# Scan mixer of a two-model stack: where its last tables and the first gated-layer weights are kept, vector additions placed between scan steps, and another tile order in the gated layer

## The reference, cut to what matters

```python
def s5_mixer(h, ...):
    u = h.reshape(b, s, 64, 16)                      # 64 groups of 16 channels
    y = y_fwd(u) + y_bwd(u) + d_skip * h             # two linear recurrences, 64 complex states per group
    g = gelu(y)
    val, gate = split(g @ w_glu, 2)                  # w_glu: 1024 x 2048
    return val * sigmoid(gate)
```

## Time and profile before

| | |
|---|---|
| time, median of 3 | 3243.75 us (3242.51 to 3245.97) |
| the profiled execution | 3244.16 us, of it the span 3242.4 us |
| PE busy | 2956.9 us (91%) |
| DVE, ACT, POOL busy | 1552.6, 1088.2, 233.1 us |
| mean granted PE clock | 0.939 of full speed |

### The profile page before, as it was taken

How to read it: one execution, slowest core, us unless ns; L and a number is a source line. 1 busy time by engine, 2 the same in 40 slices (tenths; PEclk the granted TensorE clock), 3 DMA queues, 4 the chain that set the end, 5 groups by cost and what they waited for, 6 DMA issues and landing times.

```text
span 3242.4 us, 39114 instructions
## 1 busy us (share of the span) xinstructions
PE 2956.9 (91%) x15982; PEld 2386.7 (74%) x15982; DVE 1552.6 (48%) x2302; ACT 1088.2 (34%) x1665; POOL 233.1 (7%) x216
## 2 busy tenths in 40 slices
PE   6999997479999989989999799998999998898977
PEld 5787887467888777787787478887788886665745
DVE  5776664734434334534434554344543344534444
ACT  4332333333222225525435232222332223422233
POOL 2333220100000000000000300000100000100000
PEclk9999998789999989989999799999999999987868
DMA  3244547343443221122221322222122222111000
GB/s 111 88 143 159 165 133 238 124 139 106 136 117 117 78 92 58 53 87 74 82 82 69 130 91 91 102 94 78 66 91 102 93 92 86 53 40 40 15 26 27
DMA packets 109956, 305.40 MB, mean 94 GB/s; under 512 B 27488, under 2 KB 67872, under 8 KB 80464
## 3 DMA queue, kind: packets, MB, share of 16 engines
q1 hardware_dynamic: 104656, 281.40, 26.4%
q10 hardware_dynamic: 5120, 21.50, 1.7%
HBM read 265.20 MB, written 41.85 MB: 95 GB/s over the span
## 4 chain that ended last, share of the span: by engine, by line
PE 80%; DVE 8%; ACT 3%; issue 2%; POOL 1%; DMA 1%; SPq 0%; DVEq 0%; ACTq 0%; POOLq 0%
PE ps L94 79%; DVE s_ L121 2%; PE ps L99 2%; DVE H_ L121 1%; DVE htf_ L135 1%; ACT htf_ L117 0%; ACT wh_ L117 0%; ACT hh_ L117 0%; DVE ol_ L121 0%; DVE Pm_ L121 0%; DVE nmx_ L143 0%; SPq L158 0%; ACT R_ L117 0%; DVE R_ L121 0%; DVE R_ L135 0%
## 5 line engine op out<-in xcount | busy, mean ns | idle before, releaser
L94 PE MATMUL ps<-hh_,wh_ 128*128 128x512 f32 x2184 | 870.2, 398 | 31.3 <-DVE wl_ L121 14.1
L94 PE MATMUL ps<-hl_,wh_ 128*128 128x512 f32 x2184 | 856.0, 392 | 0.0
L94 PE MATMUL ps<-hh_,wl_ 128*128 128x512 f32 x2184 | 855.1, 392 | 0.0
L121 DVE TENSOR_TENSOR wl_<-raw_,wh_ 128x2048 fp32r<-128x2048 f32 x209 | 480.3, 2298 | 558.2 <-ACT wh_ L117 558.1
L117 ACT ACTIVATE wh_<-raw_ 128x2048 fp32r<-128x2048 f32 x209 | 398.9, 1909 | 367.7 <-PE ps L94 339.7
L94 PEld LDWEIGHTS ps<-hh_,wh_ 128*128 128x128 f32 x2184 | 413.3, 189 | 131.3 <-DVE wl_ L121 14.2
L94 PEld LDWEIGHTS ps<-hh_,wl_ 128*128 128x128 f32 x2184 | 413.2, 189 | 88.1
L94 PEld LDWEIGHTS ps<-hl_,wh_ 128*128 128x128 f32 x2184 | 413.7, 189 | 87.4 <-issue 3.7
L94 PE MATMUL ps<-ah_,wl_ 128*128 128x512 f32 x704 | 279.5, 397 | 0.0
L94 PE MATMUL ps<-ah_,wh_ 128*128 128x512 f32 x704 | 278.3, 395 | 0.0
L94 PE MATMUL ps<-al_,wh_ 128*128 128x512 f32 x704 | 277.7, 395 | 0.0
(11 more groups left out here) (320 smaller groups left out, 3702.4 us busy)
## 6 DMA issues: line engine op xcount, KB each, us to landing
raw_<-in_w SPq DMA_DIRECT2D x209, 1024.0 KB, 4.9
sO<-s5ce_ SPq DMA_DIRECT2D x32, 256.0 KB, 4.0
sW<-s5wt_ SPq DMA_DIRECT2D x16, 512.0 KB, 3.7
sA<-os_ SPq DMA_DIRECT2D x24, 256.0 KB, 2.1
ol_<-sA SPq DMA_DIRECT2D x24, 256.0 KB, 3.7
sT<-sK SPq DMA_DIRECT2D x32, 128.0 KB, 3.5
sB<-mk_ SPq DMA_DIRECT2D x8, 510.0 KB, 7.6
wh_<-sW ACTq DMA_DIRECT2D x3, 1024.0 KB, 6.6
```

Source lines behind the costliest of these rows:

```text
L94: return self.e.matmul(out, lhsT, rhs, start=start, stop=stop, skip_group_check=True)
L121: return Nothing() if self.e is None else self.e.tensor_tensor(out, a, b, op)
```

## The change

It has four parts.

1. Tables 16 to 19 lie in slots 2 and 0 (`place_of`), where the lag tables 10, 11 and the tables 12, 13 were. Tables 18 and 19 are so loaded only after outputs(0) and outputs(1), by two transfers that ACT issues between its state copies. Each unit of the gated layer goes one slot further (first unit: slot 1).
2. SP loads the first two weight units into `raw0` and `raw1` as soon as same(0) and same(1) have read them, ahead of all `yx` and `yb` transfers.
3. DVE runs the first four `U` additions between the single steps of half 1: after 8, 5, 5 and 5 steps. ACT runs Gelu 0 and 1 ahead of the state copies of un = 4; Gelu 2 and 3 come behind the copies of un = 6 and 7; the two weight splits move too.
4. In the gated layer each output tile m takes value tiles k = 0..6, gate tiles k = 0..6, value tile 7, gate tile 7; the host lays the weights out in that order. Before it was value 0..7, gate 0..7. Both banks are waited for at the start of m.

```diff
+def place_of(i):
+    return i % 8 if i < 16 else i - 14
 def table_load(K, ac, i, *free):
-        ac.wait_ge(*K.at("s.used", i - 8))
+        ac.wait_ge(*K.at("s.used", i - 8 if i < 16 else i - 6))
...
 def s5_tensor(K, pe):
+        parts = [(n, b, k) for ks in (range(7), (7,)) for n, b in (("gv", bv), ("gt", bg)) for k in ks]
+        for (u, j), (name, b, k) in zip(pe.tiles(16), parts):
...
+            pe.wait_ge(*K.at("s.gl", k))
...
 def s5_scalar(K, ac, g, nxt):
-        table_load(K, ac, 16 + un)
+        if un > 1:
+            table_load(K, ac, 14 + un)
...
+        if un in (2, 3):
+            table_load(K, ac, 16 + un)
+        for n in {3: (0, 1), 6: (2,), 7: (3,)}.get(un, ()):
+            s5_gelu(K, ac, n)
+        if un == 5:
             ac.upto = len(K.units) - 1
-            ac.wait_ge(*K.at("s.used", 13))
+            ac.wait_ge(*K.at("s.used", 15))
             high(K, ac, ac.unit)
...
-    ac.wait_ge(*K.at("s.used", 15))
+    ac.wait_ge(*K.at("s.used", 17))
     high(K, ac, ac.unit + 1)
...
 def s5_vector(K, dv, g, nxt):
-    while at[1] < 64:
-        step(1)
-    bias_vector(K, dv)
     for un in range(8):
+        if un < 4:
+            for _ in range(8 if un == 0 else 5):
+                if at[1] < 64:
+                    step(1)
+        if un == 4:
+            while at[1] < 64:
+                step(1)
+            bias_vector(K, dv)
+            s5_gelu_low(K, dv, 0)
+            s5_gelu_low(K, dv, 1)
...
 def s5_sync(K, sp):
+    sp.upto = len(K.units) - 1
+    for n in range(2):
+        sp.wait_ge(*K.at("s.used", 8 + n))
+        load(K, sp, sp.unit + n)
...
-        if un in (5, 6):
-            sp.upto = len(K.units) - 1
-            sp.wait_ge(*K.at("s.used", 11 + un))
-            load(K, sp, sp.unit + un - 5)
...
-        K.slot[u] = (u - (K.first_glu if u >= K.first_glu else 0)) % SLOTS
+        K.slot[u] = (u - (K.first_glu - 1 if u >= K.first_glu else 0)) % SLOTS
```

More of the change, by code:

```diff
@@ L1087 @@
 NT = 20
+def place_of(i):
+    return i % 8 if i < 16 else i - 14
 def table(K, i):
     w = [t[:, :].bitcast(F32) for n in (2, 0, 1) for t in (K.wh[n], K.wl[n])]
-    return ([K.raw[0][:, :], K.raw[1][:, :]] + w)[i % 8]
+    return ([K.raw[0][:, :], K.raw[1][:, :]] + w)[place_of(i)]
 def table_load(K, ac, i, *free):
@@ L1105, in table_load @@
         ac.wait_ge(*K.at("p.sW", 2 * n + 1))
-    ac.dma(table(K, i), K.d[name][n]).then_inc(*K.lane(f"table{i % 8}").up("s.raw", i))
+    ac.dma(table(K, i), K.d[name][n]).then_inc(*K.lane(f"table{place_of(i)}").up("s.raw", i))
 def tables_early(K, ac, m):
@@ L1196, in s5_tensor @@
         outputs(un)
-    rhs = lambda k: (K.hh[:, k, :], K.hl[:, k, :], ("s.gl", k))
     for m in range(8):
@@ L1201, in s5_tensor @@
         pe.wait_ge(*K.after(pe, K.gb, "gv", m))
-        gemm(K, pe, bv, rhs, 8)
-        pe.mark("gv", m)
         pe.wait_ge(*K.after(pe, K.gb, "gt", m))
-        gemm(K, pe, bg, rhs, 8)
-        pe.mark("gt", m)
+        parts = [(n, b, k) for ks in (range(7), (7,)) for n, b in (("gv", bv), ("gt", bg)) for k in ks]
+        for (u, j), (name, b, k) in zip(pe.tiles(16), parts):
+            h, l = K.w(u, j)
+            if j == 0:
+                pe.wait_ge(*K.at("lo", u))
+            pe.wait_ge(*K.at("s.gl", k))
+            pe.mm(b, h, K.hh[:, k, :], k == 0, False)
+            pe.mm(b, h, K.hl[:, k, :], False, False)
+            i = pe.mm(b, l, K.hh[:, k, :], False, k == 7)
+            if k == 7:
+                i.then_inc(*pe.up(name, m))
+        pe.mark("used", u)
     pe.mark("end", "pe", "s5")
@@ L1256, in s5_scalar @@
             state_copies(K, ac, un, 1)
-        if un == 7:
+        if un in (2, 3):
[3 more added lines that the diff above has]
+        if un == 5:
             ac.upto = len(K.units) - 1
-            ac.wait_ge(*K.at("s.used", 13))
+            ac.wait_ge(*K.at("s.used", 15))
             high(K, ac, ac.unit)
[L1261 to L1266, removed]
-    ac.wait_ge(*K.at("s.used", 15))
+    ac.wait_ge(*K.at("s.used", 17))
     high(K, ac, ac.unit + 1)
-    s5_gelu(K, ac, 7)
+    for n in range(4, 8):
+        s5_gelu(K, ac, n)
     ac.wait_ge(*K.at("s.used", 19))
@@ L1362, in s5_vector @@
         if un > 5:
[L1363 to L1368, removed]
+            s5_gelu_low(K, dv, un - 4)
+    dv.deep = 2
     low(K, dv, dv.unit + 1)
-    s5_gelu_low(K, dv, 7)
+    for n in range(4, 8):
+        s5_gelu_low(K, dv, n)
     for m in range(8):
@@ L3135, in _glu @@
     g = _tiles(w[:, 1024:]).reshape(8, 8, 128, 128)
-    return _units(np.stack([v, g], 1).reshape(-1, 128, 128))
+    return _units(np.concatenate([v[:, :7], g[:, :7], v[:, 7:], g[:, 7:]], 1).reshape(-1, 128, 128))
 def _s5(I):
```

## The result

The changed kernel takes 3232.72 us (median of 8 runs, 3226.72 to 3234.92) against 3242.69 us for the kernel before in the same session (8 runs, 3237.78 to 3248.30). The ratio is 0.9967, with a 95% interval of 0.9956 to 0.9978: 10.0 us faster. The forecast was 3235.0, 3231.5 to 3240, and faster with a chance of 0.72. Sign and range held, and most of the mechanism did. Two sizes did not: what the tile order is worth, which is no term of the sum, and what happens behind the layer, where the forecast put nothing. That the number came so near is in part luck: the changed stretch gained 0.8 us less than forecast, and the time behind the layer, whose code did not change, went down too.

What follows compares the result with a forecast made beforehand. PE bounds the kernel, losing time where it waits for the gated layer's input tiles, made by SP's gathers. The layer ending 8.7 us earlier takes 3244.16 to 3235.5; that execution lay 0.4 above the median, so 3235.0, range 3231.5 to 3240.

Steps and rivals of the forecast that it cites:

- The scan's end: End of the scan on DVE: four U additions and a wait make it 3.6 us later, bounds 2.5 to 4.7.
- ACT holds outputs(4): ACT does Gelu 0 and 1 ahead of the copies for un = 4, so outputs(4) starts 5.6 us late.
- outputs(4): On PE, after the longer pause, outputs(4) takes 6.1 us instead of 5.4 and ends at 647.7, 6.3 us late.
- SP's chain: From 649.0 on SP issues the gathers of tiles 3 to 6 in 16.6 us, against 20.5 us before.
- Tile 6 and the long run: Gated layer on PE: tile 6 is ready at 669.7 and sets the end; tile 7 no longer holds PE.
- The clock in the layer: Gated layer on PE: the 366 matmuls left take 83.0 us, plus 2.3 us for lower clock.
- Rival C: PE's clock stays low or falls again in the gated layer's dense part: slower, 100 such matmuls give 3255; chance 0.06.
- B: More is gained: tile 1 in time, 2.0 us, and PE without lower clock, 2.3 us: 3230.7; chance 0.08.
- The sum: The gated layer ends at 755.0 against 763.7, so the kernel takes 8.7 us less.
- Rival A: SP's gathers are slower than counted, in tile 1 and later tiles, leaving 0.8 us of gain: 3243; chance 0.22.
- What the order is worth: In the gated layer the new tile order spares PE the stop for value tile 7, some 2.7 us.
- What follows is the same: Behind the gated layer nothing changes, as the last gate matmul is the last one in either order.

Runs made afterwards that it cites:

- e3: The changed kernel with Gelu 0 and 1 on ACT behind the state copies of un = 5, their low parts behind addition 4: 3227.99 us, ratio 0.9951.
- e9: The kernel before, unchanged, run again as a control: 3243.18 us, ratio 0.9999.
- e2: The changed kernel with the old tile order of the gated layer: 3238.06 us, ratio 0.9979.
- e7: The changed kernel with all eight U additions behind the scan and Gelu 0 and 1 behind the copies of un = 6: 3230.55 us, ratio 0.9965.
- e6: The changed kernel with the first two weight units loaded by SP between the last gathers again, their splits late: 3239.99 us, ratio 0.9986.

## Why the prediction was right, and where not

Times are counted from the first single step (611.80 before, 614.18 after).

- **The scan's end**: forecast 25.0 behind that step (+3.6), measured 24.3 (+2.9). The wait for outputs(0) was 0.94 us. The other three additions cost 0.47 us each and not 0.72: the step's series moves from 636.40 to 637.72, 1.32 us instead of 0.85, so the addition lies partly beside the operations around it. The lower bound of 2.5 was the nearer.
- **ACT holds outputs(4)**: forecast 29.8, measured 30.8. The step that was off is the gathers of tile 0, which I had let pass at 3.77 us. They took 6.24 beside tables 18 and 19, tile 1 came behind them, and both Gelus were late. I had put the delay on tile 1, whose own gathers took 3.77 and landed in 2.1 us (median). As the scan ended 0.7 us early, the wait behind its end was 1.7 us longer than forecast. That this wait would hold PE was right, and e3 shows its size: 3.5 us.
- **outputs(4)** took 5.9 us to its addition, forecast 6.1.
- **SP's chain**: forecast 16.6 us, measured 17.6 from 651.95 to 669.6 (half of the x16 row). 0.9 of the 1.0 us more is one `yx` issue of 1.32 us instead of 0.43 at 655.75. SP had no other pause, as forecast, and the additions were always in time. Such a slow issue stands in the trace of before too, in the gathers of tile 2, ahead of the 20.5 us that the forecast compared with (see the last section).
- **Tile 6 and the long run**: forecast 57.9 (669.7), measured 59.3. Tile 7 didn't hold PE.
- **The clock in the layer**: 84.76 us for 366, forecast 85.3. Granted 0.98. The low clock was worth some 1.7 us (84.76 - 366 x 0.227), where I took 2.3; the 1.9 us that the prediction reads from before are 1.8. Rival C (slower by the clock) did not occur, and B's half without a low clock neither.
- **The sum**: -8.7 forecast for the stretch, -7.9 measured (-10.3 against e9, whose own tile 7 came 1.4 us later and whose run lost 1.0 to the clock). Rival A was in part true: the gathers were slower, in another tile than I said.
- **What the order is worth**: the step that failed. 2.7 us forecast, 4.4 measured (e2). The forecast let the old order's run take 84.24 us, 1.1 less than the new one's 85.3; it took 85.27, 0.5 more than the new one's 84.76, since it too starts at the lower clock behind a pause. I charged that loss to the new order only. The term does not enter the sum, but it says which part to keep.
- **Behind the layer**: "What follows is the same" failed. The code is the same, its time is not. By the medians 10.0 us were gained, of which the stretch explains 7.9 to 10.3; the profiled executions differ by 7.9 us there. Of these 5.4 us come back in the repeats of both kernels. The stretch and these 5.4 would make 13.3 us or more, and the medians differ by 10.0, so how much of a median comes from it can't be told from single traces. The base moved as well: before was at 3243.75 us when the forecast was made and at 3242.69 in the session of the result.
- **Parts**: the early weights are worth 4.3 us, the new order 4.4, additions and Gelus -0.7 to -0.8, which is nothing within the spread. The first part (other places for the tables) has no run of its own; it is what frees `raw0` and `raw1` for the second. The forecast gave the third part a price (late outputs(4)), and by its own rows a return of 1.8 us: tile 3's gathers at 649.0 instead of 650.76. Measured against e7 the return is 0.2 us, as with the weights out of its queue SP is there nearly as early without it.

## What to carry to other kernels

When a queue is freed of one load (here the weight units on SP), work that was moved earlier to relieve it may no longer be needed; price each part with the others in place. An instruction moved ahead of the one that PE waits for brings its own wait along: the copies stood behind 3.4 us of Gelus, and behind the gathers on which these waited. And a gain of a few us should be read from the changed stretch first, with a repeat of the kernel before and after, since code behind it can differ by as much.

## What the hardware showed unexpectedly

POOL's two copies of un = 7 took 4.01 us in after and 2.22 in before; in after, as in e3, a weight split of DVE (two inputs in SBUF) runs beside them, here from 655.03:

```profile
654.45 4.01 POOL L139 COPY hf_<-H_ 64x512 f32<-64x512 f32 x2 [1.11 <-PE ps L94]
```

```profile
655.03 2.51 DVE L121 TENSOR_TENSOR wl_<-raw_,wh_ 128x2048 fp32r<-128x2048 f32 x1
```

In e6, where that split comes later, they take 2.23 us. The Trainium skill ("SBUF — State Buffer", section "Who interferes with whom") says that a DVE instruction with two SBUF inputs contends with a GpSimd instruction that reads SBUF, over a port pair that works as an exclusive lock; the traces agree. It cost PE 0.65 us ahead of outputs(7), and nothing at the end, since SP was later.

In each of the 14 traces one DMA issue of SP, at the gathers of tiles 2 to 4 and with no large transfer beside it, took 1.3 to 2.2 us instead of 0.43 (1.32 at 655.75 in after, 1.38 at 656.33 in e6, 1.45 at 646.89 in before). At each of the 14 the profile shows one transfer of 16 KB on the DMA queue that it calls `instruction`: in after the window 655.5 to 657.2 has it and 652 to 655.5 has none. So the slow issue goes with the loading of code and not with this change; where it falls moves with the order of the queue, and in after it falls on the chain. That the one causes the other no run here shows.
